# Two PSUM banks for mixed rows and two for projections in a hand-scheduled hybrid attention block, with the order of the work planned anew

## The chip, the core and the metric

The kernel runs on one core of one Trainium2 chip, as one launch. Its time is the device time in microseconds of that core, as the median of several executions. The engines are TensorE (PE, with its weight loads as PEld), VectorE (DVE), ScalarE (ACT), GpSimd (POOL) and SyncE (SP, which issues most of the DMAs).

## What is computed

One decoder block on a sequence of 2048 with width 1024: an RMS norm, a combined input projection, four groups of sequence mixers of width 512 each, a SiLU gate, an output projection, a norm and the residual.

```python
h = _rmsnorm(x, pre_norm[l])
proj = h @ w_in[l]
(a_q, a_k, a_v, sb_q, sb_k, sb_v, f_q, f_k, f_v, f_logit, m_q, gate) = jnp.split(proj, COL_SPLITS, axis=-1)
...
o_a = _diff_attention(qa, ka, va, rel_bias, lam)      # 4 heads: softmax(q0 k0) - lam * softmax(q1 k1), relative bias
o_a = _rmsnorm(o_a, diff_head_norm[l]) * (1.0 - lam_init)
o_b = _stick_breaking(...)                            # 8 heads: sigmoid and a running product over the keys
o_c = _forgetting_attention(..., log_f)               # 8 heads: softmax with a cumulated forget gate
o_m = _memory_attention(...)                          # 4 heads over 256 memory rows
y = jnp.concatenate([o_a, o_b, o_c, o_m], axis=-1) * jax.nn.silu(gate)
x = x + _rmsnorm(y @ w_out[l], post_norm[l])
```

The first three mixers are causal. The kernel keeps float32 accuracy by splitting each operand into two float16 halves (hi and lo) and multiplying three pairs of halves.

## The kernel before

**Three blocks.** A first block normalises and transposes x into `hT` and prepares the memory keys and values, the bias and the forget sums. The second, which holds nearly all the work, does the projections and all the mixers. The third multiplies the gated rows by the output weights.

**Units, lanes, steps.** The second block has 16 units: in each of four lanes one of kind forget, stick, diff and mem, in this order, each 128 columns wide (two heads of 64, or one of 128). A unit has 16 steps, one for each tile i of 128 query rows, so that there are 256 steps g. Causal rows grow: step i has (i + 1) x 128 keys, cut into chunks of up to 512, and diff has two softmaxes in each step. "Diff row 12" below is step i = 12 of a diff unit.

**A chunk's way.** PE writes its scores into one of four score banks (`scores`, L1378). For the softmax kinds DVE copies them to a ring of 11 row buffers and notes the maximum (`soft_chunk`, L1641 and L1645), which frees the bank; `peak` (L1655) joins the maxima; ACT takes the exponential (L1518). Diff then joins its two softmaxes on DVE (`combine`, L1678), after all exponentials of the step. Stick goes through two sigmoids on ACT, a scan (L1607) and a product (L1620) on DVE. ACT writes the high half (`hi`, L1496), POOL the low half (`lo`, L1574), which also frees a row buffer, and SP issues a DMA that transposes both (L1297). PE multiplies the transposed tile by the values into the mixed bank (`mix`, L1393). DVE gates the mixed row (`post`, L1731 and L1738). For diff, ACT first takes the square of the mixed row (L1510), DVE the steps of the variance (L1698 to L1705) and POOL an inverse root. `y_hi` (ACT, L1504) and `y_lo` (DVE, L1745, or POOL) split the row, and SP stores four of them at a time.

**Projection jobs.** The projections are 560 jobs (`part`, L1339): 112 of Q and K tiles (24 matmuls of 512 columns each), 192 of values and 256 of gates (24 matmuls of 128 columns each). A job fills one bank of a ring of `J_BANKS`. ACT evacuates its high half (L1443, or L1482 for a gate), then DVE its low half (L1589, or L1686), and only then does the bank come free (`j_free`). A job may be cut up into parts, with scores and mixes between them.

**Eight PSUM banks.** Four for scores, three for jobs (`j_bank`), one for mixed rows (`o_bank`). Since there is one mixed bank, the first mix of step g waits until the row of step g - 1 is posted (`pe.wait_ge(posted, g)`). The first block uses `s_bank[3]` and `j_bank[2]` as a pair for its transposes; the third uses the score banks and `j_bank[0]` and `j_bank[1]`.

**What sets the order.** Each engine runs its instructions strictly in the written order. The class `Plan` writes it: `queues` makes a queue of tasks for each kind of operation, each with its needs and an assumed length, and `run` takes over and over the task that can start first, with ties and near ties decided by the tables `RANK` and `MARGIN`. `AHEAD`, `SLACK` and `LATE` say how far the projections should be ahead of the mixers (`marks`, `behind`). That a job waits for its bank and a mix for the posted row is among the needs in the plan too, so that the number of banks changes the whole order.

Of the kernel before, what the change touches and what calls it, by code (L numbers as in the profile page):

```python
# [22 lines left out]
ACT = mybir.ActivationFunctionType  # L23
# [6 lines left out]
P = 128  # L30
# [27 lines left out]
RANK = {  # L58
    "pe": {"mix": 3.42686, "score": 5.99980, "gate": 6.18532, "project": 7.37012},
    "act": {"beta": -1.02044, "convert": 0.09860, "square": 1.56409, "y_hi": 1.90013, "stick": 4.11322,  # L60
            "job": 4.42739, "hi": 4.85840, "exp": 6.05197},
    "dve": {"lo_dve": 1.52081, "weigh": 1.69925, "ylo": 1.93750, "combine": 2.12124, "low": 2.34038,
            "post": 3.72902, "scan": 4.02979, "norm": 6.33521, "widen": 6.61046, "copy": 7.20142},
    "pool": {"lo": 0.09877, "wo": 2.26711, "ylo_pool": 2.95644, "root": 4.79189},
    "sp": {"stacks": -0.49115, "store": 1.06927, "pairs": 1.90869, "sums": 2.46883, "turn": 2.93844,
            "strip": 7.81310, "near_in": 13.10196},
}
AHEAD = {"mem": 1.00000, "stick": 0.75620, "diff": 0.14564, "forget": 0.68448}
SLACK, LATE = 17.35582, 11.80560
MARGIN = {  # L70
    "mix": 0.37422, "score": 0.17580, "gate": 0.00000, "project": 0.09693, "hi": 0.00000,
    "lo": 0.00000, "copy": 0.00000, "exp": 1.07124, "weigh": 0.00000, "norm": 1.22740,
    "y_hi": 0.53563}
DVE_LOW = {"mem": 0, "stick": 0, "diff": 0, "forget": 0}
S_BANKS, J_BANKS, PT_RING, SPLIT_RING, ROW_RING, ROWS = 4, 3, 5, 4, 11, 8
Q, K, V, G = range(4)
# [52 lines left out]
class Plan:  # L129
# [126 lines left out]
    def queues(self):  # L256
# [3 lines left out]
        for g, (t, i) in enumerate(self.steps):  # L260
# [50 lines left out]
            for at, ch in enumerate(self.t_chunks[g]):  # L311
# [13 lines left out]
                else:  # L325
# [4 lines left out]
                                  1.31, 2.7))  # L330
                need = [("turn", tau)] + ([("post", g - 1)] if g and at == 0 else [])
                if UNIT[t].has_k and at == 0:
# [265 lines left out]
def build(nc, x, mem, w_in, b_forget, w_mem_kv, w_out, pre_norm, post_norm, mem_norm,  # L598
# [27 lines left out]
    with ExitStack() as ctx:  # L626
# [7 lines left out]
        j_bank = [ctx.enter_context(nc.psum_tensor(f"job{b}", [P, BANK], F32)) for b in range(J_BANKS)]  # L634
        t_bank = [s_bank[3], j_bank[2]]
        o_bank = ctx.enter_context(nc.psum_tensor("mixed", [P, BANK], F32))

# [579 lines left out]
        with nc.Block() as block:  # L1217
# [95 lines left out]
            def _(pe):  # L1313
# [68 lines left out]
                def mix(g, tau, m, k0, tiles, first, end):  # L1382
                    unit = UNIT[plan.steps[g][0]]
                    if first and g:
                        pe.wait_ge(posted, g)
                    turned_landed(pe, tau)
                    if first and UNIT[plan.steps[g][0]].has_k:
                        pe.wait_ge(j_free, plan.job_of["v", plan.steps[g][0], V, plan.steps[g][1]][0] + 1)
                    wide = P if KINDS[g] in ("diff", "mem") else HEAD_DIM
                    v = values[unit.slot]  # L1390
                    for k in range(tiles):
                        for q, (a, b) in enumerate(((0, 0), (0, 1), (1, 0))):
                            last = nc.tensor.matmul(  # L1393
                                o_bank[:, m * HEAD_DIM:m * HEAD_DIM + wide],
                                turned[tau % PT_RING][:, (a * tiles + k) * P:(a * tiles + k + 1) * P],
                                v[:, k0 + k, b, m * HEAD_DIM:m * HEAD_DIM + wide],
                                start=(first and k == 0 and q == 0), stop=(end and k == tiles - 1 and q == 2),
                                skip_group_check=True)
                    last.then_inc(pv_done, 1)
# [24 lines left out]
            def _(act):  # L1424
# [42 lines left out]
                for op, *args in plan.orders["act"]:  # L1467
# [37 lines left out]
                    if op == "square":  # L1505
                        d = DIFF_STEP[g]
                        act.wait_ge(pv_done, mixed(g))
                        if d >= 2:
                            act.wait_ge(var_ready, (d - 1) * VAR)
                        nc.scalar.activation(junk[:, :], o_bank[:, 0:P], ACT.Square, scale=P ** -0.5,  # L1510
                                             accum_out=sc[:, 10 + d % 2:11 + d % 2]) \
                            .then_inc(squared, 1)
# [71 lines left out]
            def _(dve):  # L1584
# [135 lines left out]
                def post(g):  # L1720
# [7 lines left out]
                    if kind in ("stick", "diff"):  # L1728
                        if kind == "diff":
                            dve.wait_ge(squared, DIFF_STEP[g] + 1)  # L1730
                        nc.vector.scalar_tensor_tensor(y, o_bank[:, 0:P], 0.5 / W_SCALE if kind == "stick" else 1.0, gate,  # L1731
                                                       op0=ALU.mult, op1=ALU.mult).then_inc(posted, 1)
                        return
                    heads = 2 if kind == "forget" else 1
                    dve.wait_ge(norm_done, NORM_AT[g])
                    for h in range(heads):
                        s = slice(h * P // heads, (h + 1) * P // heads)
                        last = nc.vector.scalar_tensor_tensor(y[:, s], o_bank[:, s], rz[:, g % 2, h:h + 1], gate[:, s],  # L1738
                                                              op0=ALU.mult, op1=ALU.mult)
# [162 lines left out]
```

## Time and profile before

| | us |
|---|---|
| median of 3 runs | 2605.59 |
| lowest and highest | 2602.4, 2607.44 |
| the profiled execution | 2597.89 |
| span of its instructions | 2596.1 |
| PE, DVE, ACT, POOL busy | 2344.3, 1676.6, 1598.9, 1348.5 |

The mean granted TensorE clock is 0.97 of full speed. The 1.8 us between the span and the execution's time lie outside the instructions. The profiled execution is one of several, and stands 7.7 us below the median. Matmuls overlap one another: a single one is shown with its latency (0.22 us for 128 columns) while the next starts after a quarter of that, so a group's duration from its first start to its last end is what can be read.

### The profile page before, as it was taken

What the parts mean: (1) busy time and instruction counts of PE and PEld (TensorE: products, weight loads), DVE (VectorE), ACT (ScalarE), POOL (GpSimd) and SP (SyncE); (2) the same over time, 40 slices, a digit from 0 to 9 for tenths busy, and PEclk for the clock granted to TensorE, in tenths of its full rate; (3) what the DMA queues carried; (4) which work ended last, traced back from release to release, by engine and by line L of the source; (5) the groups of instructions that cost most, each with busy time, mean ns of one, the idle gap of its engine ahead of it and who ended that gap; (6) DMA issues with size and microseconds to landing.
All of it is one profiled execution on the core that took longest, in us unless ns stands there. A gap on an engine that the chain in (4) does not pass through costs nothing. (4 is left out here: it accounts for less than half of the span.)

```text
span 2596.1 us, 71707 instructions
## 1 busy us (share of the span) xinstructions
PE 2344.3 (90%) x26710; PEld 1597.2 (62%) x26710; DVE 1676.6 (65%) x4701; ACT 1598.9 (62%) x4309; POOL 1348.5 (52%) x2128
## 2 busy tenths in 40 slices
PE   5699999998999999969999999699999995899998
PEld 4476676656766666558666665486666663644443
DVE  7646699876556997765559987656489885311111
ACT  5457888665568885655688866557788765312211
POOL 6435555776565566765655667756656565100000
PEclk9799999998999999989999999899999997899999
DMA  6359989645599887455998874567988833854341
GB/s 198 96 120 158 164 159 157 137 91 111 130 179 174 161 143 160 88 99 126 179 171 157 143 164 92 101 129 153 180 160 151 160 75 61 209 147 114 81 114 49
DMA packets 987798, 353.00 MB, mean 136 GB/s; under 512 B 833956, under 2 KB 972204, under 8 KB 987436
## 3 DMA queue, kind: packets, MB, share of 16 engines
q1 hardware_dynamic: 980856, 330.58, 65.2%
q0 software_dynamic: 6592, 17.83, 2.6%
q8 instruction: 210, 3.44, 0.5%
q14 instruction: 140, 1.15, 0.1%
HBM read 72.38 MB, written 35.23 MB: 41 GB/s over the span
## 5 line engine op out<-in xcount | busy, mean ns | idle before, releaser
L1574 POOL TENSOR_TENSOR rows<-rows 128x512 f16<-128x512 f32 (+3 forms) x864 | 867.5, 1020 | 646.7 <-ACT rows L1496 640.2
L1339 PE MATMUL job<-wt,big 128*128 128x128 f16 x10752 | 686.5, 220 | 0.8 <-DVE planes L1589 0.4
L1339 PE MATMUL job<-big,wt 128*128 128x512 f16 x2688 | 663.2, 380 | 8.2 <-PEq L760 5.1
L1339 PEld LDWEIGHTS job<-wt,big 128*128 128x128 f16 x10752 | 630.8, 98 | 46.0 <-DVE gate_s L1686 0.7
L1496 ACT CAST rows<-rows 128x512 f16<-128x512 f32 (+3 forms) x864 | 459.1, 545 | 215.0 <-DMA rows<-rows 171.4
L1393 PEld LDWEIGHTS mixed<-values,rows 128*128 128x128 f16 x8544 | 384.9, 100 | 216.5 <-DMA rows<-rows 107.1
L1393 PE MATMUL mixed<-values,rows 128*128 128x64 f16 (+1 forms) x8544 | 440.6, 202 | 83.4 <-DMA rows<-rows 63.7
L1378 PE MATMUL scores<-stack 128*128 128x512 f16 (+3 forms) x1600 | 435.5, 352 | 63.3 <-DVE mx L1645 42.8
L1518 ACT ACTIVATE rows<-rows,neg_max 128x512 f32<-128x512 f32 (+3 forms) x704 | 445.5, 634 | 76.2 <-DVE neg_max L1655 76.0
L1641 DVE TENSOR_SCALAR_CACHE_REDUCE rows<-scores 128x512 f32<-128x512 f32 (+3 forms) x640 | 360.3, 582 | 121.6 <-POOL rows L1574 92.6
L1339 PEld LDWEIGHTS job<-big,wt 128*128 128x128 f16 x2688 | 246.8, 98 | 257.7 <-issue 9.0
L1607 DVE TENSOR_TENSOR_SCAN temps<-temps,scores 128x512 f32<-128x512 f32 (+3 forms) x320 | 346.9, 1089 | 35.5 <-ACT scores L1465 29.4
L1378 PEld LDWEIGHTS scores<-stack 128*128 128x128 f16 x1600 | 132.1, 98 | 160.6 <-DVE mx L1645 48.2
L1620 DVE TENSOR_TENSOR rows<-scores,temps 128x512 f32<-128x512 f32 (+4 forms) x320 | 185.9, 601 | 6.6 <-DVE temps L1607 0.9
L1453 ACT ACTIVATE temps<-scores 128x512 f32<-128x512 f32 (+3 forms) x320 | 167.4, 539 | 24.3 <-DVE rows L1620 19.9
L1465 ACT ACTIVATE scores<-scores 128x512 f32<-128x512 f32 (+3 forms) x320 | 165.4, 535 | 2.7
L1857 DVE TENSOR_TENSOR sc<-sc 128x1 f32<-128x1 f32 x16 | 2.5, 159 | 250.7 <-ACT rows L1842 192.7
L1842 ACT ACTIVATE rows<-scores 128x512 f32<-128x512 f32 x22 | 12.9, 592 | 201.2 <-PE scores L1831 147.8
L1518 ACT ACTIVATION_READ_ACCUMULATOR rows<-rows,neg_max 128x1 f32 x704 | 132.8, 189 | 0.0
L1589 DVE SCALAR_TENSOR_TENSOR planes<-job,planes 128x512 f16<-128x512 f32 x112 | 76.5, 683 | 82.1 <-ACT planes L1443 81.9
L1482 ACT ACTIVATE gate_t<-job 128x128 f32<-128x128 f32 x256 | 70.7, 278 | 89.5 <-PE job L1339 83.6
L1678 DVE SCALAR_TENSOR_TENSOR rows<-rows,sc 128x512 f32<-128x512 f32 (+3 forms) x160 | 118.8, 783 | 2.3
(155 smaller groups left out, 2630.7 us busy)
## 6 DMA issues: line engine op xcount, KB each, us to landing
stack<-planes SPq DMA_DIRECT2D x160, 192.0 KB
ws<-w_in SPq DMA_DIRECT2D x56, 512.0 KB, 4.7
y_halves<-y_out_halves SPq DMA_DIRECT2D x64, 256.0 KB, 2.7
rows<-rows SPq DMA_TRANSPOSE x864, 3.3
rows<-x SPq DMA_DIRECT2D x16, 512.0 KB, 5.2
temps<-w_out POOLq DMA_DIRECT2D x64, 128.0 KB, 3.6
out_weight_halves<-temps POOLq DMA_DIRECT2D x64, 128.0 KB, 3.8
big<-out_weight_halves SPq DMA_DIRECT2D x16, 512.0 KB, 10.9
```

What stands on the lines that cost most here:

```text
L1339: last = nc.tensor.matmul(dst, lhs, rhs, start=(k0 == 0 and q == 0), stop=(k1 == KT and q == len(pairs) - 1))
L1378: last = nc.tensor.matmul(bank[:, at:at + width], lhs, rhs, start=(q == 0), stop=(q == len(parts) - 1), skip_group_check=True)
L1393: last = nc.tensor.matmul(o_bank[:, m * HEAD_DIM:m * HEAD_DIM + wide], turned[tau % PT_RING][:, (a * tiles + k) * P:(a * tiles + k + 1) * ...
L1453: nc.scalar.activation(slot(n, w), s_bank[n % S_BANKS][:, 0:w], ACT.Sigmoid, scale=-1.0) \
L1465: nc.scalar.activation(z, z, ACT.Sigmoid).then_inc(stick_beta, 1)
L1496: nc.scalar.copy(halves_of(tau, 0, w), scored(n, 0, w)).then_inc(split_hi, 1)
L1518: nc.scalar.activation(mine, mine, ACT.Exp, bias=neg_max[:, r:r + 1], accum_out=z_part[:, r, c // BANK:c // BANK + 1]) \
L1574: nc.gpsimd.tensor_tensor(halves_of(tau, 1, w), scored(plan.chunk_at(g, m, k0), 0, w), halves_of(tau, 0, w), ALU.subtract).then_inc(low_po ...
L1607: nc.vector.tensor_tensor_scan(out=u[:, ::-1], data0=u[:, ::-1], data1=s_bank[n % S_BANKS][:, 0:w], initial=1.0 if first else temps[:, aft ...
L1620: nc.vector.tensor_tensor(mine, s_bank[n % S_BANKS][:, 0:keys], temps[:, after:after + keys], ALU.mult) \
L1641: last = nc.vector.tensor_scalar(scored(n, a, b), s_bank[n % S_BANKS][:, a:b], 1.0, -3.0e38, ALU.mult, ALU.max, accum_out=peak)
L1678: nc.vector.scalar_tensor_tensor(first, second, sc[:, 1:2], first, op0=ALU.mult, op1=ALU.add) \
```

## The change

The mixed rows get two banks, `o_banks`, used in turn by step; the jobs have two banks and not three. A first mix waits for the row two steps back, in the plan and in the code. The first block's second pair of transposes goes to the second mixed bank. Since two mixed rows can now be alive, the square of a diff row waits for the square before it, because both write `junk`. All the numbers of the planner's tables are new (a line of them is shown), and so is the order on every engine.

```diff
 RANK = {
-    "pe": {"mix": 3.42686, "score": 5.99980, "gate": 6.18532, "project": 7.37012},
+    "pe": {"mix": 3.83100, "score": 4.71205, "gate": 6.18532, "project": 8.20302},
...
-S_BANKS, J_BANKS, PT_RING, SPLIT_RING, ROW_RING, ROWS = 4, 3, 5, 4, 11, 8
+S_BANKS, J_BANKS, O_BANKS, PT_RING, SPLIT_RING, ROW_RING, ROWS = 4, 2, 2, 5, 4, 11, 8
...
-                need = [("turn", tau)] + ([("post", g - 1)] if g and at == 0 else [])
+                need = [("turn", tau)] + ([("post", g - O_BANKS)] if g >= O_BANKS and at == 0 else [])
...
-        t_bank = [s_bank[3], j_bank[2]]
-        o_bank = ctx.enter_context(nc.psum_tensor("mixed", [P, BANK], F32))
+        o_banks = [ctx.enter_context(nc.psum_tensor(f"mixed{b}", [P, BANK], F32)) for b in range(O_BANKS)]
+        o_bank = o_banks[0]
+        t_bank = [s_bank[3], o_banks[1]]
...
-                    if first and g:
-                        pe.wait_ge(posted, g)
+                    if first and g >= O_BANKS:
+                        pe.wait_ge(posted, g - O_BANKS + 1)
...
-                                o_bank[:, m * HEAD_DIM:m * HEAD_DIM + wide],
+                                o_banks[g % O_BANKS][:, m * HEAD_DIM:m * HEAD_DIM + wide],
...
                         d = DIFF_STEP[g]
+                        if d:
+                            act.wait_ge(squared, d)
                         act.wait_ge(pv_done, mixed(g))
```

The reads of the mixed bank in `square` and `post` change in the same way. Lines of the kernel after are one (PE) or three (DVE) higher than those of before.

Three places of the new order. The first is PE at the end of the diff unit of lane 1, from the last scores of diff row 15 on (`scores<-stack` are diff's, `scores<-values,planes` mem's; `job<-big,wt` of 512 columns is a part of a Q or K job, `job<-wt,big` of 128 one of a value or gate job). Before:

```order
L1378 MATMUL scores<-stack 128x512 x4
L1339 MATMUL job<-wt,big 128x128 x24
L1378 MATMUL scores<-stack 128x512 x2
L1393 MATMUL mixed<-values,rows 128x128 x12
L1378 MATMUL scores<-values,planes 128x256 x18
L1393 MATMUL mixed<-values,rows 128x128 x12
L1378 MATMUL scores<-values,planes 128x256 x3
```

After, from the same scores on:

```order
L1379 MATMUL scores<-stack 128x512 x2
L1340 MATMUL job<-big,wt 128x512 x9
L1340 MATMUL job<-wt,big 128x128 x24
L1340 MATMUL job<-big,wt 128x512 x12
L1379 MATMUL scores<-stack 128x512 x2
L1379 MATMUL scores<-values,planes 128x256 x3
L1340 MATMUL job<-big,wt 128x512 x3
L1379 MATMUL scores<-values,planes 128x256 x3
L1340 MATMUL job<-big,wt 128x512 x3
L1394 MATMUL mixed<-values,rows 128x128 x12
L1379 MATMUL scores<-values,planes 128x256 x3
L1394 MATMUL mixed<-values,rows 128x128 x12
```

Before, one narrow gate job stands there. After, wide jobs stand ahead of diff's last scores and between mem's.

The second is PE a little later, where the last diff rows are mixed and the first mem rows follow. Before:

```order
L1393 MATMUL mixed<-values,rows 128x128 x21
L1339 MATMUL job<-wt,big 128x128 x24
L1378 MATMUL scores<-values,planes 128x256 x3
L1393 MATMUL mixed<-values,rows 128x128 x48
L1339 MATMUL job<-wt,big 128x128 x36
L1393 MATMUL mixed<-values,rows 128x128 x6
L1339 MATMUL job<-wt,big 128x128 x36
L1393 MATMUL mixed<-values,rows 128x128 x6
```

After:

```order
L1340 MATMUL job<-big,wt 128x512 x3
L1394 MATMUL mixed<-values,rows 128x128 x9
L1340 MATMUL job<-big,wt 128x512 x3
L1340 MATMUL job<-wt,big 128x128 x24
L1340 MATMUL job<-big,wt 128x512 x24
L1379 MATMUL scores<-values,planes 128x256 x3
L1340 MATMUL job<-wt,big 128x128 x24
L1340 MATMUL job<-big,wt 128x512 x15
L1394 MATMUL mixed<-values,rows 128x128 x12
L1340 MATMUL job<-big,wt 128x512 x3
L1394 MATMUL mixed<-values,rows 128x128 x12
L1340 MATMUL job<-big,wt 128x512 x3
```

Here 27 wide and 24 narrow matmuls, and then more wide ones by threes, stand among the mixes, where before only narrow ones stood. A narrow job now follows a wide one, and is followed by one, with nothing else between them.

The third is DVE in diff rows 12 and 13 of lane 3. Before, from one post (L1731) to the copies behind the combine (L1678):

```order
L1731 SCALAR_TENSOR_TENSOR y_f<-mixed,gate_s 128x128
L1698 TENSOR_SCALAR sc<-z_sum 128x1
L1701 TENSOR_SCALAR sc<-sc 128x1
L1703 TENSOR_SCALAR root_i<-sc 128x1
L1705 TENSOR_SCALAR root_i<-root_i 128x1
L1661 TENSOR_REDUCE z_sum<-z_part 128x2
L1672 RECIPROCAL sc<-z_sum 128x1
L1674 TENSOR_SCALAR sc<-sc,neg_lam,z_sum 128x1
L1678 SCALAR_TENSOR_TENSOR rows<-rows,sc 128x512 x3
L1678 SCALAR_TENSOR_TENSOR rows<-rows,sc 128x256
L1686 SCALAR_TENSOR_TENSOR gate_s<-gate_t,job 128x128
L1745 SCALAR_TENSOR_TENSOR y_out_halves<-y_f,root,y_out_halves 128x128
```

After, from the combine's first step on (L1664, which was L1661):

```order
L1664 TENSOR_REDUCE z_sum<-z_part 128x2
L1675 RECIPROCAL sc<-z_sum 128x1
L1677 TENSOR_SCALAR sc<-sc,neg_lam,z_sum 128x1
L1681 SCALAR_TENSOR_TENSOR rows<-rows,sc 128x512 x3
L1681 SCALAR_TENSOR_TENSOR rows<-rows,sc 128x256
L1734 SCALAR_TENSOR_TENSOR y_f<-mixed,gate_s 128x128
L1701 TENSOR_SCALAR sc<-z_sum 128x1
L1704 TENSOR_SCALAR sc<-sc 128x1
L1706 TENSOR_SCALAR root_i<-sc 128x1
L1708 TENSOR_SCALAR root_i<-root_i 128x1
L1644 TENSOR_SCALAR rows,mx<-scores 128x128
L1648 ISA rows,mx<-scores,near_f 128x256
```

The post of the earlier row and the four steps of its variance stood ahead of the combine, and now stand behind it, in front of the copies; `y_lo` (L1745) and the gate step (L1686) no longer stand between the combine and the first copy.

## Rows read from the trace of the kernel before

**Rows 1.** The page's first part: engine, busy us (share of the span), instructions.

```profile
span 2596.1 us, 71707 instructions
PE 2344.3 (90%) x26710; PEld 1597.2 (62%) x26710; DVE 1676.6 (65%) x4701; ACT 1598.9 (62%) x4309; POOL 1348.5 (52%) x2128
```

**Rows 2.** Groups by line on PE: busy, mean ns, idle before, releasers.

```profile
L1339 PE MATMUL job<-wt,big 128*128 128x128 f16 x10752 | 686.5, 220 | 0.8 <-DVE planes L1589 0.4 <-DVE gate_s L1686 0.4
L1393 PE MATMUL mixed<-values,rows 128*128 128x64 f16 (+1 forms) x8544 | 440.6, 202 | 83.4 <-DMA rows<-rows 63.7 <-issue 17.0 <-DVE y_f L1738 1.3
```

**Rows 3.** Busy time by stretch: us, engines, granted clock, DMA share, GB/s.

```profile
core 0: us, PE busy (x) PEld busy (x) DVE busy (x) ACT busy (x) POOL busy (x), PEclk, DMA share, GB/s
...
538.00:631.00 93.00, 79.66 (x688) 50.72 (x687) 62.50 (x202) 52.22 (x143) 65.11 (x130) 0.93 0.50 96
631.00:664.50 33.50, 33.50 (x512) 30.39 (x510) 19.72 (x93) 19.35 (x69) 19.11 (x35) 1.00 0.60 120
664.50:814.00 149.50, 141.38 (x1937) 102.98 (x1935) 90.29 (x323) 102.07 (x284) 97.99 (x113) 1.00 0.84 159
814.00:979.00 165.00, 158.93 (x2176) 112.35 (x2175) 145.71 (x230) 140.61 (x361) 95.08 (x103) 1.00 0.89 160
979.00:1065.00 86.00, 80.14 (x829) 53.54 (x826) 69.33 (x277) 51.63 (x154) 58.65 (x148) 0.98 0.68 137
1065.00:1157.50 92.50, 71.56 (x650) 47.60 (x648) 61.55 (x200) 53.06 (x147) 64.78 (x129) 0.87 0.49 92
...
1596.60:1689.40 92.80, 70.60 (x645) 47.44 (x643) 61.21 (x200) 52.80 (x146) 65.18 (x131) 0.89 0.48 93
...
2042.70:2120.70 78.00, 75.18 (x802) 51.36 (x801) 66.36 (x272) 49.91 (x152) 42.76 (x129) 1.00 0.59 114
2120.70:2210.80 90.10, 56.72 (x524) 39.95 (x522) 55.74 (x188) 48.74 (x138) 45.42 (x97) 0.75 0.37 67
```

**Rows 4.** Groups on PE by shape, from 1065.3 to 1157.4 us.

```profile
L1339 PE MATMUL job<-big,wt 128*128 128x512 f16 x111 | 26.1, 379 | 0.0
...
L1339 PE MATMUL job<-wt,big 128*128 128x128 f16 x179 | 11.6, 220 | 0.0
```

**Rows 5.** Timeline of PE: start us, duration, what [idle before <-releaser].

```profile
1121.10 1.50 PE L1339 MATMUL job<-wt,big 128*128 128x128 f16 x24
1133.05 1.03 PE L1378 MATMUL scores<-stack 128*128 128x512 f16 x2 [10.45 <-DVE mx L1645]
...
1135.16 3.80 PE L1378 MATMUL scores<-values,planes 128*128 128x256 f16 x18
...
1147.14 0.82 PE L1378 MATMUL scores<-values,planes 128*128 128x256 f16 x3 [4.68 <-DVE rows L1641]
```

**Rows 6.** Timeline of all engines in diff row 14 of lane 3.

```profile
2175.44 1.50 PE L1339 MATMUL job<-wt,big 128*128 128x128 f16 x24
...
2175.72 0.29 DVE L1731 SCALAR_TENSOR_TENSOR y_f<-mixed,gate_s 128x128 f32<-128x128 f32 x1 [3.47 <-ACT junk L1510]
...
2177.48 0.26 ACT L1482 ACTIVATE gate_t<-job 128x128 f32<-128x128 f32 x1
2177.61 0.16 DVE L1661 TENSOR_REDUCE z_sum<-z_part 128x2 f32<-128x8 f32 x1 [0.86 <-ACT rows L1518]
...
2180.84 0.28 DVE L1686 SCALAR_TENSOR_TENSOR gate_s<-gate_t,job 128x128 f32<-128x128 f32 x1
...
2182.33 0.57 DVE L1745 SCALAR_TENSOR_TENSOR y_out_halves<-y_f,root,y_out_halves 128x128 f16<-128x128 f32 x1 [1.21 <-ACT y_out_halves L1504]
```

**Rows 7.** Timeline where a value job is evacuated by engines that stood waiting.

```profile
663.70 0.28 ACT L1443 ACTIVATE values<-job 128x128 f16<-128x128 f32 x1 [0.28 <-PE job L1339]
...
664.01 0.29 DVE L1589 SCALAR_TENSOR_TENSOR values<-job,values 128x128 f16<-128x128 f32 x1 [0.18 <-ACT values L1443]
```

**Rows 8.** Timeline of PE, a Q or K job without interruption.

```profile
525.33 5.34 PE L1339 MATMUL job<-big,wt 128*128 128x512 f16 x24
```

More of the change, by code:

```diff
@@ L58 @@
 RANK = {
-    "pe": {"mix": 3.42686, "score": 5.99980, "gate": 6.18532, "project": 7.37012},
[L60 to L66, printed above, removed]
-}
-AHEAD = {"mem": 1.00000, "stick": 0.75620, "diff": 0.14564, "forget": 0.68448}
-SLACK, LATE = 17.35582, 11.80560
+    "pe": {"mix": 3.83100, "score": 4.71205, "gate": 6.18532, "project": 8.20302},
+    "act": {"convert": 0.55415, "beta": 1.83717, "y_hi": 1.90013, "job": 2.17791, "stick": 4.11322,
+            "hi": 4.85840, "exp": 6.63861, "square": 7.61772},
+    "dve": {"ylo": 0.19770, "combine": 2.32931, "weigh": 2.42837, "low": 3.29298, "post": 3.92919,
+            "scan": 4.39958, "lo_dve": 4.81384, "copy": 5.13532, "norm": 5.79374, "widen": 9.40558},
+    "pool": {"lo": 0.37655, "wo": 2.56825, "ylo_pool": 2.95644, "root": 6.07821},
+    "sp": {"stacks": -0.49115, "store": 1.32939, "sums": 2.46792, "turn": 3.30809, "strip": 3.54526,
+            "pairs": 7.01523, "near_in": 14.26105},
+}
+AHEAD = {"mem": 0.88912, "stick": 0.75620, "diff": 0.14564, "forget": 0.77018}
+SLACK, LATE = 16.65695, 11.97694
 MARGIN = {
-    "mix": 0.37422, "score": 0.17580, "gate": 0.00000, "project": 0.09693, "hi": 0.00000,
-    "lo": 0.00000, "copy": 0.00000, "exp": 1.07124, "weigh": 0.00000, "norm": 1.22740,
-    "y_hi": 0.53563}
+    "mix": 0.70567, "score": 0.17580, "gate": 0.00000, "project": 0.08517, "hi": 0.00000,
+    "lo": 0.00000, "copy": 0.00000, "exp": 0.12751, "weigh": 0.07014, "norm": 1.22740,
+    "y_hi": 0.37523}
 DVE_LOW = {"mem": 0, "stick": 0, "diff": 0, "forget": 0}
-S_BANKS, J_BANKS, PT_RING, SPLIT_RING, ROW_RING, ROWS = 4, 3, 5, 4, 11, 8
+S_BANKS, J_BANKS, O_BANKS, PT_RING, SPLIT_RING, ROW_RING, ROWS = 4, 2, 2, 5, 4, 11, 8
 Q, K, V, G = range(4)
@@ L1509, in _ @@
                             act.wait_ge(var_ready, (d - 1) * VAR)
-                        nc.scalar.activation(junk[:, :], o_bank[:, 0:P], ACT.Square, scale=P ** -0.5,
+                        nc.scalar.activation(junk[:, :], o_banks[g % O_BANKS][:, 0:P], ACT.Square, scale=P ** -0.5,
                                              accum_out=sc[:, 10 + d % 2:11 + d % 2]) \
@@ L1730, in post @@
                             dve.wait_ge(squared, DIFF_STEP[g] + 1)
-                        nc.vector.scalar_tensor_tensor(y, o_bank[:, 0:P], 0.5 / W_SCALE if kind == "stick" else 1.0, gate,
+                        nc.vector.scalar_tensor_tensor(y, o_banks[g % O_BANKS][:, 0:P], 0.5 / W_SCALE if kind == "stick" else 1.0, gate,
                                                        op0=ALU.mult, op1=ALU.mult).then_inc(posted, 1)
@@ L1737, in post @@
                         s = slice(h * P // heads, (h + 1) * P // heads)
-                        last = nc.vector.scalar_tensor_tensor(y[:, s], o_bank[:, s], rz[:, g % 2, h:h + 1], gate[:, s],
+                        last = nc.vector.scalar_tensor_tensor(y[:, s], o_banks[g % O_BANKS][:, s], rz[:, g % 2, h:h + 1], gate[:, s],
                                                               op0=ALU.mult, op1=ALU.mult)
```

## The prediction

> **What bounds the kernel now.** I read the page first, for busy shares. TensorE (PE) is busy 2344.3 of 2596.1 us, VectorE (DVE) and ScalarE (ACT) 65% and 62% [rows 1]. PE seems to be the bound, but a share over the whole span can hide a stretch in which another engine is. So next the groups by line: is PE ever held by a projection bank or by the mixed bank? Hardly. In front of the 10752 narrow projection matmuls it was idle 0.8 us in all; in front of the mixed-row matmuls 83.4 us, of which 63.7 for a transposed tile to land and 1.3 for the posted row (DVE y_f) [rows 2]. The bank that the change adds was therefore not waited for in the order as it was written. What it may bring, it brings by another order.
>
> So the third view is the table by stretch, cut at the points where a unit's scores begin [rows 3]. Each lane runs forget, stick, diff, mem. In the forget, stick and early diff rows of lane 1 PE is busy 141.4 of 149.5, 158.9 of 165.0 and 80.1 of 86.0 us: there it bounds, with DVE close behind in stick (145.7 of 165.0). From the scores of diff row 12 to the first mix of mem it is not: 79.7 of 93.0, 71.6 of 92.5, 70.6 of 92.8 and 56.7 of 90.1 us in the four lanes, with granted clocks of 0.93, 0.87, 0.89 and 0.75. The reader is to see that these four last about the same, 90 to 93 us, whatever PE has to do in them. That is the mark of a stretch whose length another chain sets. I call it the dry stretch.
>
> The timeline of lane 1's dry stretch shows how [rows 5]. PE finishes a gate job at 1122.60 us and then sits 10.45 us in front of diff scores, released by a DVE copy that frees the score bank, later 4.68 us more. After the first hole it runs at half the clock: 18 matmuls of 256 columns took 3.80 us. The chain is copies of a row, peak, eight exps, combine, hi, lo, and the copies of the next row, which need ring space that lo frees; no projection or mixed bank is in it.
>
> **The change part by part.** *Filler in the dry stretches* is the term that carries the forecast. The work is the same in total (560 jobs); what counts is where it stands. In lane 1's dry stretch before there are 111 projection matmuls of 512 columns and about 180 of 128 [rows 4]. Counted in the written orders between the same two points (scores of diff row 12, first mix of mem), lanes 1 and 2 have 168 and 228 after, lane 0 has 183 and 192 after 156 and 180 (and 18 mixes less), lane 3 has 48 after 15 of the wide kind. A wide one costs (5.34 - 0.38) / 23 = 0.216 us, a narrow one (1.50 - 0.22) / 23 = 0.056 us [rows 2, 4, 5, 8]. So lanes 1 and 2 get 57 x 0.216 + 48 x 0.056 = 15.0 us each, lane 0 27 x 0.216 + 12 x 0.056 - 18 x 0.056 = 5.5, lane 3 33 x 0.216 = 7.1: 42.6 us in all. The order excerpts show the place: wide jobs now stand between the last diff scores and the mem scores, and among the mixes behind them, just where PE had its two holes. There is room: 92.5 - 71.6 = 20.9 us of plain idleness in lane 1, before the slow clock is counted.
>
> These 42.6 us leave other stretches. By the same count lanes 1 and 2 lose about 9.7 us each in diff rows 0 to 11 (129 and 384 matmuls become 75 and 420) and 4.0 each in stick (72 narrow ones fewer). Early diff is PE's at 80.1 of 86.0 us, and in lane 3 the same rows took 78.0 us, so the other chains allow at least 8 us less: I count 8 of 9.7. In stick DVE has only 19.3 us of its own left in 165.0 and waits on PE, ACT and rings in turn: I count 2 of 4. Lane 0's jobs go mostly past the dry stretch into the first mem rows (15 us more there, all PE time, 33.5 of 33.5) out of the following forget (12 less, PE 141.4 of 149.5): with what stick, early diff and the dry part give I count 3 for the lane. Lane 3 gives up 7 us that all ends in its own dry stretch; I count 5. Sum: 10 + 10 + 3 + 5 = 28 us saved. The bounds are 0 (other chains take it all) and 42.6.
>
> *The clock.* With fewer holes the granted clock in the dry stretches should rise. Of 3.80 us for 18 matmuls of 256 columns about half is clock, and a few such groups per lane lie between a hole and the first mem mix. That part is at the same time on the way to the next copies, so I count 3 us over four lanes, between 0 and 10.
>
> *Two projection banks, not three.* A job may start only when the job two back is evacuated by ACT and then DVE. At best this takes 0.60 us from ACT's start, which stood waiting for PE, to DVE's end [rows 7]; with exps queued on ACT and a combine on DVE it took from 2176.94 to 2181.12, 4.2 us [rows 6]. In the order after, 55 jobs of 558 have nothing between them and the job two back but one narrow job of 24 matmuls, 1.35 us. Before, with three banks, 22 of 557 had only two such jobs (2.7 us), and the whole wait seen was 0.8 us [rows 2]. If half of the 55 meet a busy ACT or DVE and wait 0.6 us, that is 16 us; but those in a dry stretch cost nothing, and the order knows of the ring. I take 9 us lost. The bounds are 0 and, if each of the 55 waits for 2.85 us more (4.2 - 1.35), 157, which nothing in the profile makes likely; a tenth of a microsecond on each of 558 jobs would be 56.
>
> *Mixed rows in two banks.* The wait on the previous posted row goes; it was 1.3 us [rows 2], and is 0 for the sum. On DVE in the late diff rows, post and the variance steps stand behind combine and not ahead of it. Before, DVE sat 3.47 us ahead of post, but after it and the variance steps DVE waited 0.86 us more for the exps that combine needs, so post was not what held combine [rows 6]. The steps take 2177.61 - 0.86 - 2175.72 = 1.03 us a row; now they stand between combine and the copies, where they may lie on the chain that sets the dry stretch; y_lo has left the same place, which held 1.21 us of waiting [rows 6]. I call it 0, between -3 and +3 us. The new wait of ACT's square is for the square of the diff row before, which a whole row of work lies behind, and the preamble's transposes only use another bank: 0. The Q and K jobs of the next forget unit end 9.0 to 9.3 us of PE work ahead of its first scores, after 9.7 to 10.0 in the same count before, so SP's stack loads are at most 0.7 us later in the program: 0, at worst 2.
>
> A rule speaks against a gain. The Trainium skill (TensorE: Matmul & The Clock Gate, HAM oscillation) reports for a matmul kernel that, once PE was kept fed, double-buffering PSUM gave no further gain, 125.5 against 126.6 us. The trace agrees so far as the mixed bank was hardly waited for; by that rule alone the time would stay.
>
> **Sum.** 28 + 3 - 9 = 22 us less. The profiled execution took 2597.89 us (span 2596.1), so it would take 2576. The median of the three runs is 2605.59, 7.7 above that execution; the same step from the median gives 2583.6.
>
> **Rivals.** *No change (within 0.2%, 5 us, which is about what a measurement of this kernel can tell).* The stretches that give up work are then held by DVE and by the transposes' landing: the mixes wait 63.7 us for them at 94% PE [rows 2], and a mix that comes earlier waits longer. If a third of 28 is realised, 9 us, the bank waits eat it: 2600 to 2611. For it: the landing waits are spread over all units. Against: early diff took 78.0 us in lane 3.
>
> *Slower: the projection ring becomes a wait.* Its place is the mem and forget rows, where narrow jobs follow one another and each job holds PE back until ACT and DVE have come round. It decides from 31 us of waits, 0.056 us for each of 558 jobs. At 0.1 us each, 56 us, with the 31 gained, the time is 2631. For it: three banks had hidden evacuations of up to 4.2 us, and two jobs' distance is now often 1.35. Against: the order leaves more than 2 us of other work in front of most jobs.
>
> *More: the filler counts in full.* 42.6, and 8 for the clock, with 5 of ring waits: 46 less, 2560; for it, the dry stretches' constant length.
>
> **How the numbers follow.** Forecast (2570 to 2598) 0.50, more 0.14, no change 0.14, slower 0.22. Faster by over 0.2% is 0.64, within 0.14, slower 0.22. The range takes in the full filler with the clock's bound (2550) and the slow rival's 2631, leaving a little below one in ten at each end.
>
> **What would show it.** In the profile after: the four dry stretches still last 88 to 93 us, with PE at 78 to 85 in lanes 1 and 2 and a clock above 0.93; the hole of 10.45 us in front of the diff scores under 6; early diff in lanes 1 and 2 at 77 to 80 us; idleness in front of the projection matmuls grown from 0.8 to about 10 us. The forecast is wrong if that idleness is over 30 us, if the dry stretches grow with their filler, or if early diff keeps its 86 us because the mixes then wait for transposes.

## The result

The changed kernel takes 2578.76 us as the median of 4 runs (2575.15 to 2583.14); before, run beside it, takes 2606.52 (2602.4 to 2607.83, 4 runs). The ratio is 0.9904, with a 95% interval of 0.9889 to 0.9919: 25 us faster, between 21 and 29. The forecast was 2584, in a range of 2550 to 2631. The profiled execution of the change took 2575.15 us, with a span of 2573.3, 22.8 less than before's.

The page of the change, first part (as [rows 1]):

```profile
span 2573.3 us, 71706 instructions
PE 2342.4 (91%) x26710; PEld 1587.3 (62%) x26710; DVE 1666.9 (65%) x4701; ACT 1590.7 (62%) x4309; POOL 1341.0 (52%) x2128
```

PE's busy time is the same within 2 us. The 22.8 us are idle time that is gone. Where PE is idle now, by line (as [rows 2]; busy us, mean ns, idle before, releasers), first what waits for a job's bank, then mixes and scores:

```profile
L1340 PE MATMUL job<-wt,big 128*128 128x128 f16 x10752 | 689.9, 219 | 14.5 <-DVE planes L1592 5.0 <-DVE gate_s L1689 4.6 <-DVE values L1592 3.7
L1340 PE MATMUL job<-big,wt 128*128 128x512 f16 x2688 | 668.6, 383 | 28.0 <-DVE planes L1592 18.1 <-PEq L761 5.1 <-DVE wt L1598 2.9
L1394 PE MATMUL mixed<-values,rows 128*128 128x64 f16 (+1 forms) x8544 | 433.7, 200 | 70.4 <-DMA rows<-rows 55.1 <-issue 12.4 <-DVE y_f L1741 1.6
L1379 PE MATMUL scores<-stack 128*128 128x512 f16 (+3 forms) x1600 | 432.4, 351 | 39.7 <-DVE mx L1648 18.5 <-DVE rows L1623 11.0 <-DVE rows L1644 4.4
```

The narrow job matmuls were held 0.8 us before [rows 2] and are held 14.5 now; the wide ones 8.2 before (in the same answer as rows 2) and 28.0 now. That is 33.5 us more in front of jobs. In front of mixes it is 13.0 us less [rows 2], in front of diff's and the other stacked scores 23.6 less than the 63.3 of before, and in front of mem's scores 8.0 after 26.5.

The change by stretch, cut at the same points of the program as [rows 3]: dry and first mem rows of lane 0; forget, stick, early diff and dry of lane 1; dry of lane 2; early diff and dry of lane 3.

```profile
core 0: us, PE busy (x) PEld busy (x) DVE busy (x) ACT busy (x) POOL busy (x), PEclk, DMA share, GB/s
...
537.30:618.60 81.30, 80.08 (x706) 50.03 (x707) 58.11 (x186) 51.15 (x138) 59.29 (x122) 1.00 0.57 112
618.60:669.10 50.50, 50.39 (x763) 45.07 (x761) 28.36 (x119) 24.55 (x86) 26.34 (x48) 1.00 0.49 114
669.10:810.60 141.50, 131.03 (x1729) 91.91 (x1727) 85.98 (x304) 98.17 (x273) 94.51 (x111) 0.99 0.89 160
810.60:978.30 167.70, 157.81 (x2103) 108.56 (x2104) 145.19 (x227) 138.69 (x356) 95.22 (x103) 1.00 0.88 158
978.30:1054.70 76.40, 68.91 (x811) 49.44 (x810) 64.28 (x267) 48.81 (x150) 51.87 (x127) 1.00 0.69 129
1054.70:1151.60 96.90, 84.19 (x750) 52.53 (x747) 63.31 (x216) 55.36 (x156) 63.09 (x142) 0.96 0.52 103
...
1578.80:1674.80 96.00, 82.17 (x749) 52.23 (x747) 63.65 (x216) 55.35 (x156) 64.06 (x142) 0.98 0.53 104
...
2027.30:2103.40 76.10, 73.70 (x835) 53.14 (x833) 63.95 (x273) 49.65 (x152) 40.98 (x118) 0.98 0.66 115
2103.40:2186.80 83.40, 58.52 (x556) 39.92 (x553) 57.16 (x198) 50.46 (x143) 45.66 (x108) 0.86 0.39 73
```

Early diff of lane 1 fell from 86.0 to 76.4 us, a little further than forecast. But the dry stretches did not keep their 90 to 93 us: those of lanes 1 and 2 grew to 96.9 and 96.0, those of lanes 0 and 3 shrank to 81.3 and 83.4. In sum they are some 10 us shorter, with 42.6 us more of PE's work in them. Here is the end of lane 1's, where [rows 5] had holes of 10.45 and 4.68 us:

```profile
1126.15 0.84 PE L1394 MATMUL mixed<-values,rows 128*128 128x128 f16 x12 [1.32 <-DMA rows<-rows]
...
1128.96 1.50 PE L1340 MATMUL job<-wt,big 128*128 128x128 f16 x24
1132.49 7.04 PE L1340 MATMUL job<-big,wt 128*128 128x512 f16 x24 [2.03 <-DVE planes L1592]
1139.37 0.49 PE L1379 MATMUL scores<-values,planes 128*128 128x256 f16 x3
1139.70 1.50 PE L1340 MATMUL job<-wt,big 128*128 128x128 f16 x24
```

The holes are filled by wide jobs, and what is left is a job's own wait for its bank: the narrow job before it ends at 1130.46, and the wide one starts 2.03 us later, when DVE has evacuated the job two back.

### The profile page after: what moved, and what is told of

The parts are those of the page before. It is cut to its first block and busy times, and to the rows that moved or that the text cites. A ratio compares the mean times of both kernels' runs of the same rounds, so it can differ in the third digit from the quotient of the medians.

```text
span 2573.3 us, 71706 instructions
## 1 busy us (share of the span) xinstructions
PE 2342.4 (91%) x26710; PEld 1587.3 (62%) x26710; DVE 1666.9 (65%) x4701; ACT 1590.7 (62%) x4309; POOL 1341.0 (52%) x2128
## 5 line engine op out<-in xcount | busy, mean ns | idle before, releaser
L1340 PE MATMUL job<-wt,big 128*128 128x128 f16 x10752 | 689.9, 219 | 14.5 <-DVE planes L1592 5.0
L1394 PE MATMUL mixed<-values,rows 128*128 128x64 f16 (+1 forms) x8544 | 433.7, 200 | 70.4 <-DMA rows<-rows 55.1
L1689 DVE SCALAR_TENSOR_TENSOR gate_s<-gate_t,job 128x128 f32<-128x128 f32 x256 | 71.8, 282 | 79.1 <-ACT gate_t L1483 78.3
```

The costliest lines, as they stand in the source:

```text
L1340: last = nc.tensor.matmul(dst, lhs, rhs, start=(k0 == 0 and q == 0), stop=(k1 == KT and q == len(pairs) - 1))
L1394: last = nc.tensor.matmul(o_banks[g % O_BANKS][:, m * HEAD_DIM:m * HEAD_DIM + wide], turned[tau % PT_RING][:, (a * tiles + k) * P:(a * til ...
```

## The experiments

A ratio is always to before, run beside the kernel. The table of all, and then the sets.

| kernel | job banks, mixed banks | tables | us | ratio (95%) |
|---|---|---|---|---|
| the change | 2, 2 | new | 2578.76 | 0.9904 (0.9889 to 0.9919) |
| e1 | 2, 2 | old | 2619.42 | 1.006 (1.0043 to 1.0077) |
| e2 | 3, 1 | new | 2580.19 | 0.9897 (0.9877 to 0.9917) |
| e3 | 2, 1 | old | 2640.42 | 1.0137 (1.012 to 1.0153) |
| e4 | 2, 2, in the order for 3, 1 | old | 2636.9 | 1.0117 (1.0099 to 1.0136) |
| e5 | 2, 1 | new | 2611.44 | 1.0034 (1.002 to 1.0049) |
| e6 | 3, 1 | new RANK | 2582.23 | 0.9912 (0.9891 to 0.9933) |
| e7 | 3, 1 | new MARGIN | 2601.04 | 0.999 (0.9979 to 1.0001) |
| e8 | 2, 2 | new, old AHEAD, SLACK, LATE | 2602.32 | 0.9995 (0.9983 to 1.0008) |
| e9 | 3, 1 | old, filler moved | 2594.82 | 0.9962 (0.9947 to 0.9976) |
| e10 | 3, 1 | new, filler moved | 2569.45 | 0.9854 (0.9833 to 0.9875) |
| e11 | 3, 1 | new RANK on DVE | 2608.68 | 1.0004 (0.9991 to 1.0016) |
| e12 | 3, 1 | new RANK on ACT, SP | 2588.29 | 0.993 (0.9914 to 0.9946) |

Before is 3, 1 with the old tables. Its median in these sets was 2602.46 to 2607.0.

### Banks and tables apart (e1 to e4)

e1 takes the change and puts the tables back:

```diff
-RANK = { ... of the change }
+RANK = { ... of before }
-AHEAD, SLACK, LATE, MARGIN of the change
+AHEAD, SLACK, LATE, MARGIN of before
```

> The banks of the change (two for jobs, two for mixed rows), the order planned for them, but all planner tables as before. Three theories. Filler: the time follows how much projection work stands in the four dry stretches (diff row 12 to the first mem mix); this order has 45, 48, 45 and 28 us of it there in lanes 0 to 3, before had 44, 34, 34 and 12, after 50, 49, 49 and 19. So it gains most of what the change gained: 2577 to 2592. Tables: the gain came from the new numbers; then 2600 to 2625, since two job banks alone only add waits. Mixed ring: the gain is that a mix need not wait for the posted row; then about 2580 to 2590 too, and the third kernel of this set tells it from filler.

It took 2619.42 us, 14 more than before (16 by the ratio). The order has the filler, and the time is not there.

e2 is the other half:

```diff
-S_BANKS, J_BANKS, O_BANKS, ... = 4, 2, 2, ...
+S_BANKS, J_BANKS, O_BANKS, ... = 4, 3, 1, ...
-        t_bank = [s_bank[3], o_banks[1]]
+        t_bank = [s_bank[3], j_bank[2]]
```

> Three job banks and one mixed bank as before, but the planner tables of the change. Its dry stretches hold 47, 31, 34 and 16 us of projection work, about as before (44, 34, 34, 12). Filler: within 6 us of before, 2600 to 2612. Tables: the whole gain, 2575 to 2590. Mixed ring: as before, 2600 to 2612.

It took 2580.19 us, 25 less than before (27 by the ratio), and the same as the change within 2 us. With this my filler theory fell as the cause of the gain: this order has hardly more filler than before's (128 us after 124, in sum over the dry stretches).

e3 has two job banks and one mixed bank, with the old tables:

```diff
-S_BANKS, J_BANKS, O_BANKS, ... = 4, 2, 2, ...
+S_BANKS, J_BANKS, O_BANKS, ... = 4, 2, 1, ...
-        t_bank = [s_bank[3], o_banks[1]]
+        spare = ctx.enter_context(nc.psum_tensor("spare", [P, BANK], F32))
+        t_bank = [s_bank[3], spare]
```

> Two job banks, one mixed bank (the eighth bank only serves the transposes of the first block), planner tables as before. Its dry stretches hold 49, 44, 44 and 22 us of projection work. Filler: faster than before, 2580 to 2595, with over 20 us of waits in front of jobs and four dry stretches of 85 to 96 us. Mixed ring: no faster than before, 2606 to 2625, as a bank was taken away and none given. Tables: 2606 to 2625.

It took 2640.42 us, 35 more than before and 21 more than e1, although it has filler too. So the second mixed bank is worth 21 us with the old tables; I had priced it at nothing.

e4 keeps before's order on every engine and runs it on the new banks:

```diff
+PLAN_J, PLAN_O = 3, 1
...
-                need = [("turn", tau)] + ([("post", g - O_BANKS)] if g >= O_BANKS and at == 0 else [])
+                need = [("turn", tau)] + ([("post", g - PLAN_O)] if g >= PLAN_O and at == 0 else [])
...
-                    if name in ("gate", "project") and jobs >= J_BANKS:
-                        bank = end.get(("j_free", jobs - J_BANKS))
+                    if name in ("gate", "project") and jobs >= PLAN_J:
+                        bank = end.get(("j_free", jobs - PLAN_J))
```

> The order of before word for word on every engine, run with two job banks and two mixed banks. It leaves the filler where it was and adds only the ring's waits. In the trace of before, 121 jobs opened before the job two back was evacuated, by 107 us in sum, part of it in idle stretches. All theories: slower; I expect 2635 to 2680, waits in front of jobs of 40 to 90 us, and mixed rows waiting no less than before. If it is within 10 us of before, the ring's waits are absorbed elsewhere and my term for them means nothing.

It took 2636.9 us, 31 more than before. Its groups on PE:

```profile
L1341 PE MATMUL job<-wt,big 128*128 128x128 f16 x10752 | 691.4, 220 | 40.8 <-DVE planes L1593 17.7 <-DVE gate_s L1690 12.6 <-DVE values L1593 9.1
L1341 PE MATMUL job<-big,wt 128*128 128x512 f16 x2688 | 664.3, 381 | 31.2 <-DVE planes L1593 14.3 <-DVE gate_s L1690 6.4 <-PEq L762 5.1
L1395 PE MATMUL mixed<-values,rows 128*128 128x64 f16 (+1 forms) x8544 | 439.3, 202 | 53.5 <-DMA rows<-rows 37.7 <-issue 14.2
```

The waits in front of jobs grew by 40.0 + 23.0 = 63 us, and the mixes' wait fell by 30. Of that, 26 are waits for a transposed tile (37.7 us after 63.7), while a transpose takes 3.3 us from issue to landing in both kernels: a PE that comes later finds it landed. So half of this ring wait is given back elsewhere. Most of the 31 us that stay lost are in the stick stretches, which took 173.9, 175.5, 175.1 and 171.4 us where before took 167.4, 164.8, 168.9 and 168.3.

### Which table, and what the second mixed bank is worth (e5 to e8)

e5 is the change without its second mixed bank:

```diff
-S_BANKS, J_BANKS, O_BANKS, ... = 4, 2, 2, ...
+S_BANKS, J_BANKS, O_BANKS, ... = 4, 2, 1, ...
-        t_bank = [s_bank[3], o_banks[1]]
+        spare = ctx.enter_context(nc.psum_tensor("spare", [P, BANK], F32))
+        t_bank = [s_bank[3], spare]
```

> Two job banks and one mixed bank with the planner tables of the change: the change without its second mixed bank. With the old tables the second mixed bank was worth 21 us (2640.4 without, 2619.4 with). If that is a property of the bank, this takes about 2600 (2592 to 2608) where the change takes 2578.8; if the new tables also stand in for the bank, 2575 to 2588.

It took 2611.44 us. These kernels were timed in different sets, and before's median differs by up to 5 us between the sets, so I compare ratios. Without the mixed bank the change loses 0.0130, 34 us (1.0034 after 0.9904). Against e2, which has a third job bank, e5 loses 0.0137, 36 us. Each of the two is known to about 6 us. So with the new tables the job bank that the change gives up and the mixed bank that it gets are worth about the same, and cancel. What is left is the tables' gain, 27 us with the old banks (e2).

By the same reckoning the tables are worth 27 us with two job banks and one mixed (e5 after e3), and 41 with two and two (the change after e1). With the old tables the change of banks alone costs 16 us (e1), with the new ones nothing. So no part has one price that holds beside all the others.

Of the 27.3 us between the profiled spans of e5 and the change, 19 lie in early diff (333.6 us in sum over the lanes, 314.4 in the change).

e6 and e7 are before with one table of the change each:

```diff
-    "act": {"beta": -1.02044, "convert": 0.09860, "square": 1.56409, ...
+    "act": {"convert": 0.55415, "beta": 1.83717, ... "square": 7.61772},
...
```

for e6 (and so on for the other engines), and for e7

```diff
 MARGIN = {
-    "mix": 0.37422, ... "project": 0.09693, ... "exp": 1.07124, "weigh": 0.00000, ...
+    "mix": 0.70567, ... "project": 0.08517, ... "exp": 0.12751, "weigh": 0.07014, ...
```

> Banks, MARGIN, AHEAD, SLACK and LATE as before; only RANK (the priorities among tasks on an engine) is the change's. The filler theory has fallen with the second run of the first set; now the question is which table carries its 25 us. If the priorities do: 2576 to 2590, and this kernel's early diff stretches are as short as there. If the margins do (above all exp, 1.07 to 0.13, so that exps are taken earlier): 2598 to 2612.

> Banks, RANK, AHEAD, SLACK and LATE as before; only MARGIN is the change's. If the margins carry the gain: 2576 to 2592, with early diff rows shorter by 15 us in sum over the lanes, since exps come sooner on ACT and they are on the chain from copies to combine. If the priorities carry it: 2598 to 2612. Both at about half: neither table alone does it.

e6 took 2582.23 us (0.9912), e7 2601.04 (0.999, no difference that the interval shows). With the old banks the priorities carry it: 23 of e2's 27 us. AHEAD, SLACK and LATE put into before's tables by themselves leave its order as it is, on every engine. What they do with the old banks beside the new priorities and margins was not run.

e8 puts AHEAD, SLACK and LATE back in the change:

```diff
-AHEAD = {"mem": 0.88912, "stick": 0.75620, "diff": 0.14564, "forget": 0.77018}
-SLACK, LATE = 16.65695, 11.97694
+AHEAD = {"mem": 1.00000, "stick": 0.75620, "diff": 0.14564, "forget": 0.68448}
+SLACK, LATE = 17.35582, 11.80560
```

> The change with AHEAD, SLACK and LATE as before, which moves projection work: the dry stretches hold 40, 41, 41 and 26 us where the change has 50, 49, 49 and 19, early diff 51, 44, 44 and 39 where it has 44, 40, 40 and 44. If filler is worth what I priced it at (0.65 of the work moved): 19 us moved out of lanes 0 to 2, 7 into lane 3, so 8 us slower than the change, 2583 to 2591. If filler is worth nothing: 2575 to 2582.

It took 2602.32 us, 24 more than the change, three times what I expected. In lanes 1 and 2 the dry stretches fell to 86.9 and 87.0 us and early diff rose to 81.8 and 81.5; in lane 0, early diff took 98.0 us where the change has 84.1. So the loss is not one of filler by the us, and this run does not say what else in its order costs it. It does say that on the new banks the priorities and margins are not enough: with them alone the kernel is as fast as before (0.9995), and all of its gain comes only with AHEAD, SLACK and LATE.

### Filler by itself, and the priorities by engine (e9 to e12)

e9 moves only filler, in before's own kernel:

```diff
                 need = [("w", t, kind)]
+                if what == "qk" and not unit.has_k and index:
+                    need.append(("score", self.chunks[(t - 1) * nt + 12][0][0]))
```

> The kernel before with one need more in the plan: the last three Q jobs of a mem unit may not start until diff row 12's first scores have run. That moves 12 us of projection matmuls from early diff into the dry stretch in each of lanes 1 to 3, and 2 to 3 us in lane 0; banks and tables stay. Priced as in the prediction (early diff is PE's, the dry stretch's length is another chain's): 0.65 of 39 us, 25 us faster, about 2578; early diff 10 us shorter in each of three lanes, dry stretches unchanged within 2 us. If the dry stretch is not elastic in that way and grows with what is put in: early diff shorter and dry longer by the same, 2598 to 2608. The runs with other tables and old banks, which gained without filler, make me give each half.

It took 2594.82 us: 0.9962, 10 us, where 25 was the price. Its early diff and dry stretches of lane 1, and early diff of lanes 2 and 3:

```profile
982.70:1064.90 82.20, 68.88 (x759) 46.96 (x760) 65.67 (x268) 49.60 (x149) 56.73 (x141) 0.98 0.67 136
1064.90:1160.20 95.30, 83.77 (x711) 54.01 (x711) 62.38 (x206) 54.26 (x150) 64.43 (x140) 0.91 0.46 94
...
1513.00:1595.30 82.30, 67.70 (x763) 46.01 (x761) 66.45 (x272) 50.09 (x150) 57.90 (x143) 0.99 0.69 139
...
2040.70:2117.30 76.60, 66.31 (x764) 46.38 (x761) 63.77 (x270) 48.11 (x148) 40.90 (x127) 0.99 0.61 117
```

The dry stretches take the filler nearly free: 369.8 us in sum over the lanes after 368.1, for some 39 us of matmuls put in. What fails is the other side. Some 37 us were taken from early diff, and it became 8.2 us shorter (326.1 after 334.3 in sum). PE is now busy 68.9 of 82.2 us in lane 1's. It had been busy 93% of that stretch, but another chain stood only some 4 us behind it: PE now waits 8.1 us there for score banks that DVE's copies free, after 0.2 in before.

e10 is the same need with the new tables, that is e2 with e9's edit:

```diff
-S_BANKS, J_BANKS, O_BANKS, ... = 4, 2, 2, ...
+S_BANKS, J_BANKS, O_BANKS, ... = 4, 3, 1, ...
...
+                if what == "qk" and not unit.has_k and index:
+                    need.append(("score", self.chunks[(t - 1) * nt + 12][0][0]))
```

> Old banks, the change's tables, and the same extra need for the Q jobs of mem: 16 to 19 us moved into the dry stretch in lanes 1 and 2, 12 in lane 3. If filler and priorities are two separate gains they add: 2580.2 less 15 to 25, 2555 to 2565, faster than the change. If the filler only trades one stretch for another: 2575 to 2585.

It took 2569.45 us, ratio 0.9854: the two gains add (0.0103 and 0.0038 alone, 0.0146 together), and it beats both kernels, with the banks of before. But filler adds 11 us to e2's gain, not the 15 to 25 that I expected. Its early diff stretches of lanes 0, 2 and 3:

```profile
455.40:532.00 76.60, 71.58 (x820) 50.97 (x820) 65.56 (x264) 51.17 (x152) 52.12 (x122) 1.00 0.75 146
...
1504.60:1585.30 80.70, 62.69 (x658) 41.47 (x656) 62.51 (x255) 47.14 (x140) 50.87 (x118) 0.96 0.67 131
...
2031.50:2100.50 69.00, 61.05 (x660) 40.19 (x661) 60.64 (x252) 45.10 (x138) 36.19 (x102) 1.00 0.65 116
```

In sum early diff took 306.0 us after 316.8 in e2, and the dry stretches 366.7 after 361.6. So here too much less is gained in early diff than is moved out of it (some 49 us).

e11 and e12 split RANK by engine:

> The kernel before with the change's priorities on DVE alone (copy ahead of norm and widen, low behind the gating steps). All priorities together gave 2582.2 with these banks. If DVE's carry it, because the copies that free score banks no longer stand behind weight conversion and variance in the late diff rows: 2580 to 2590, dry stretches shorter by 10 us or more in sum. If not: 2598 to 2610.

> The complement: the kernel before with the change's priorities on ACT and SP alone (square and exp later, job evacuation earlier, weight strips earlier). If DVE's carry the gain: 2598 to 2610; if ACT's and SP's do: 2580 to 2590; with each carrying half, 2590 to 2598.

```diff
-    "dve": {"lo_dve": 1.52081, "weigh": 1.69925, "ylo": 1.93750, ... "norm": 6.33521, "widen": 6.61046, "copy": 7.20142},
+    "dve": {"ylo": 0.19770, "combine": 2.32931, "weigh": 2.42837, ... "copy": 5.13532, "norm": 5.79374, "widen": 9.40558},
```

for e11, and for e12

```diff
-    "act": {"beta": -1.02044, "convert": 0.09860, "square": 1.56409, "y_hi": 1.90013, ... "job": 4.42739, ... "exp": 6.05197},
+    "act": {"convert": 0.55415, "beta": 1.83717, "y_hi": 1.90013, "job": 2.17791, ... "exp": 6.63861, "square": 7.61772},
-    "sp": {... "pairs": 1.90869, ... "strip": 7.81310, "near_in": 13.10196},
+    "sp": {... "strip": 3.54526, "pairs": 7.01523, "near_in": 14.26105},
```

DVE's priorities gave nothing (1.0004). ACT's and SP's gave 0.993, 18 of the 23 us of all priorities. PE's and POOL's were not run apart. The trace shows one thing that ACT's do. In before's diff rows ACT's square stood in the middle of the next row's exps. The timeline of ACT in before, the same row of lane 3 as [rows 6]:

```profile
2172.30 0.71 ACT L1518 ACTIVATE rows<-rows,neg_max 128x512 f32<-128x512 f32 x1
2172.91 0.19 ACT L1518 ACTIVATION_READ_ACCUMULATOR rows<-rows,neg_max 128x1 f32 x1
2175.21 0.28 ACT L1510 ACTIVATE junk<-mixed 128x128 f32<-128x128 f32 x1 [2.11 <-PE mixed L1393]
2175.38 0.19 ACT L1510 ACTIVATION_READ_ACCUMULATOR junk<-mixed 128x1 f32 x1
2175.47 0.71 ACT L1518 ACTIVATE rows<-rows,neg_max 128x512 f32<-128x512 f32 x1
```

The square waits 2.11 us for PE's mixed row, and three exps wait behind it. With `"square": 7.61772` it stands behind them. In e12 the eight exps of the same row are not held by it; the last three of them:

```profile
2171.35 0.71 ACT L1521 ACTIVATE rows<-rows,neg_max 128x512 f32<-128x512 f32 x1
2171.96 0.19 ACT L1521 ACTIVATION_READ_ACCUMULATOR rows<-rows,neg_max 128x1 f32 x1
2172.05 0.71 ACT L1521 ACTIVATE rows<-rows,neg_max 128x512 f32<-128x512 f32 x1
2172.67 0.19 ACT L1521 ACTIVATION_READ_ACCUMULATOR rows<-rows,neg_max 128x1 f32 x1
2172.76 0.60 ACT L1521 ACTIVATE rows<-rows,neg_max 128x384 f32<-128x384 f32 x1
2173.26 0.19 ACT L1521 ACTIVATION_READ_ACCUMULATOR rows<-rows,neg_max 128x1 f32 x1
```

The eight take from 2169.57 to 2177.58 in before, 8.0 us, and from 2167.63 to 2173.45 in e12, 5.8. The list of waits says the same for the whole run: DVE's post behind ACT's square, in before, and then in e12 (us, times, longest):

```profile
DVE y_f L1731 <- ACT junk L1510: 57.9, 22, 10.1
```

```profile
DVE y_f L1734 <- ACT junk L1513: 8.2, 9, 1.4
```

In the change it is 3.9 us.

The written orders say how often this happens. In before, 14 of the 64 squares stand between two exps of one row, all in diff rows 11 to 14. In e12 it is 2, in e6 1, in e2 and the change none. In e7 and e11, which gained nothing, it is 21 and 20. But e8 has none either and is no faster than before, on the other banks.

The dry stretches took 354.1 us in sum in e12 after 368.1, 14 us less, and 352.0 in e6; in e11 they took 370.3. The 14 us are not a share of the 18: the profiled execution of e12 is 8.6 us shorter than before's (span 2587.5), with the stick stretches 10 us longer and early diff 7 us shorter. That the square's place alone makes the 18 us was not tried, since ACT's other priorities and SP's went with it. ACT's alone already give e12's order on PE, ACT, DVE and POOL, so that SP's change only SP's order; this kernel was not run either.

## Why the prediction was right, and where it was not

The direction and the size were right, 22 us forecast and 25 by the ratio, and the time lies 5 us under the forecast. But it came out of terms that were wrong in both directions, and that they met so near the measured time is luck.

**Filler, 28 us.** Its mechanism was right in one half. The dry stretches take added matmuls nearly free (e9: +1.7 us for 39 put in). The step that failed is "Early diff is PE's at 80.1 of 86.0 us": I counted 8 of 9.7 us saved there. e9 took 37 us out and gained 10. In the change early diff did become 20 us shorter (314.4 after 334.3), with some 28 us of jobs taken out. But in e2 it became 17 shorter (316.8) with 4 taken out, and in e5 less than 1 (333.6) with 8 taken out: the jobs in it do not set its length by themselves. The support that I found for it, lane 3's 78.0 us, was no support: in lane 3 POOL is busy 42.8 us, in lane 1 58.7 [rows 3], since the output weights are prepared in the first three lanes alone. That this is why lane 3 is shorter was not tested. At e9's rate, 10 us for 39 put in, the 42.6 us moved are worth 11, which is an estimate.

**What I did not see: the priorities, 23 us with the old banks (e6).** The prediction read in [rows 6] that combine waited 0.86 us for exps, and stopped there with "post was not what held combine". The question after that was what held the exps, and the answer, ACT's square, was one row away. The square waits for PE's mixed row, so the dry stretch's chain, which I had written down without it, did have a mixed row in it. This is what e12 points to, and new tables alone (e2) bring all that the change brings. In the change itself they do so only together with AHEAD, SLACK and LATE, which are worth 24 us there (e8).

**Two job banks, 9 us.** The sign was right and the size was not. Waits in front of jobs grew by 33.5 us, over the 30 that I had named as the mark of being wrong, and giving up the bank costs 36 us by the ratios (e5 against e2). Between those two the waits grew by 26 (38.6 after 12.3). Some 18 of the 33.5 us lie in the dry stretches of lanes 1 and 2 (7.3 and 11.1 us), where I had said that they cost nothing; those stretches grew by 4.4 and 3.2 us, which is the second mark that I had named.

**Two mixed banks, 0 us.** Wrong: 34 us with the new tables, 21 with the old. The step that failed is "The wait on the previous posted row goes; it was 1.3 us, and is 0 for the sum". A wait that the written order avoids is not seen in the trace; what it cost lay in the order that avoided it. Which of the mixes that the second bank lets the planner move bring the gain was not tried.

**The clock, 3 us.** The granted clock of the dry stretches rose from 0.93, 0.87, 0.89, 0.75 [rows 3] to 1.00, 0.96, 0.98, 0.86. What that was worth by itself no run tells.

Along one path, from before by e2 and e5 to the change, the parts are 27 us gained for the tables, 36 lost for the job bank and 34 gained for the mixed bank. Their sum is the measured 25 by construction, since each step starts where the last one ends; it confirms nothing, and by another path the parts have other sizes (e1: 16 lost for the banks, then 41 gained for the tables). Filler has no place of its own in it; part of what banks and tables do is to move it.

The rival of no change expected the mixes to wait longer for their transposes; they waited 8.6 us less (55.1 after 63.7). The Trainium skill (TensorE: Matmul & The Clock Gate, HAM oscillation) reports that double-buffering PSUM gave its matmul kernel no further gain. That agrees with the change of banks as a whole here, with the new tables (e2 against the change, 2580.2 and 2578.8), but not with the mixed bank, which taken by itself is worth 34 us. The 94% PE that this rival takes from [rows 2] is not in those rows; the nearest are 141.4 of 149.5 us in [rows 3], 95%. The slow rival's mechanism is real: it was to decide from 31 us of waits (0.056 us for each of 558 jobs), and 33.5 were measured. The time fell all the same, by gains that the prediction had not priced.

## What to carry to other kernels

A written order hides the price of the resources that shaped it: a ring on which 1.3 us of waiting is seen can be worth 34 us, and only a run with another ring and a new order shows it. Where a change moves banks and planner numbers together, run the four corners, and do not add their differences as if each part had one price. Here the numbers alone gave all of the gain, and the numbers with filler moved, on the old banks, gave more than the change.

A share of 93% busy does not say how far behind the next chain stands; taking some work out of the stretch does. And when an engine waits 0.86 us for another, look at what that one waited for in the middle of the same row.

## What the hardware showed that I had not expected

A late PE gives back half of what holds it: in e4, 63 us more of waits in front of jobs came with 30 us less in front of mixes, as transposes that take as long as before (3.3 us) are met later. And the granted clock was no guide to the time: e1 ran with a mean clock of 0.979 to 0.980 and e3 with 0.974 to 0.979, where before had 0.967 to 0.970 beside them, and they are 14 and 35 us slower.
